# Two modulation slabs at a time between the matmuls of a four-block transformer kernel

## The chip, the cores and the metric

The kernel runs on one core of a Trainium2 chip as one program. The metric is the device time of one execution in microseconds (us); the number given for a kernel is the median of its runs. The engines of the core named below are TensorE (PE, with its weight loads as PEld), VectorE (DVE), ScalarE (ACT), GpSimd (POOL) and SyncE (SP), which here only starts the weight transfers.

## What is computed

Two models of two transformer blocks each, one behind the other, on 256 tokens of 1024 features and a context of 256 more tokens. Every block has an adaptive modulation: a vector `silu(c)` of 1024 numbers for the tokens, and one for the context, is multiplied by a matrix of 1024 x 6144, and the six parts of the result shift, scale and gate what the block does. This product is the subject of the change.

```
def modulation(cvec, w_mod, b_mod):
    m = (jax.nn.silu(cvec) @ w_mod + b_mod).reshape(-1, 1, N_MOD * D_MODEL)
    return jnp.split(m, N_MOD, axis=-1)
...
        x = x + g1 * heads_out(att_x, px, hy, w_out[l])
        x = x + g2 * sq_relu_mlp(modulate(rms_norm(x, norm2_g[l]), sh2, sc2), w_mlp1[l], w_mlp2[l])
...
        mod_x = jnp.split((jax.nn.silu(c) @ ada_w[i] + ada_b[i])[:, None, :], 6, axis=-1)
```

The first model mixes tokens by latent attention (8 heads), a Fourier transform and a long convolution; the second by a gated delta rule and then by gated linear attention. Each block ends in an MLP of 1024 to 4096 to 1024 with a squared ReLU. All is float32.

## The kernel before

**Weights in slabs.** Every weight matrix is cut on the host into slabs of 128 x 2048 float32 (1 MB: 1024 rows by 256 columns), laid in one array in the order in which they are used. SP brings them one after the other into a ring of four places (`ring`, `RING = 4`). In `slabs` the transfer of slab n waits until `n - RING + 2` slabs are begun, that is until slab n-3 has been begun: PE counts `slab_begun` up with the first matmul of each slab, and by then it is through with slab n-4, whose place the new one takes. So when a slab is begun, the transfer of the third slab after it may start.

**Own slabs.** An ordinary product goes in three matmuls (`three_products`, L763 to L765): weights and data are each split into a rounded part and a rest, since the fast format rounds. ACT makes the rounded part of a slab (`w_high`, L1411 in the MLP), DVE the rest (L1894), and only then PE may begin it (`w_split`). In the MLP of both token sets a slab is 48 matmuls of 128x512. ACT makes the rounded part of own slab j+1 only after PE is through with own slab j-1, whose buffer it takes. An MLP runs in four quarters of eight own slabs, 0 to 3 being of the first matrix and 4 to 7 of the second.

**Hosted slabs.** The slabs of the modulation are of another kind. `pe_slab_rows` (L955 to L965; its matmul is L960) multiplies a slab unsplit with two vectors only: eight matmuls, each on 32 columns of the array and in its own quarter of them (`tile_position=(0, r)`). The profile counts each as two, since they are full float32. Four slabs fill one PSUM bank (6); ACT copies it (L1337, L1434), PE turns it (`pe_turn_rows`, L969), DVE adds it up (L976). These slabs depend on nothing near, so they are hosted by other stages. Who hosts them:

- The attention of both blocks of the first model (`pe_attn`), with 24 slabs in its 32 units and 16 slabs in its 16 units (`woven`). A unit is one head and 128 queries: scores of unit i (L990), one hosted slab while i < m, transposes of the probabilities of unit i-2 (L1004), and at even i the products with the values of a pair of units (L1015); at every fourth i also the turn (L969). DVE takes the row minimum (L1735), ACT the exponentials (L1330), DVE scales (L1742), ACT copies the transposes (L1346). In the first 16 units the scores are 512 wide, in the other 16 of the first block 256 wide.
- The MLP of the first block and the MLP behind the delta rule (`hosts`), each with 24 slabs, eight behind the own slabs of each of its first three quarters by `HOSTED`. `mlp_slab` counts where in the ring's order own slab j stands, and `mlp_slabs` on the host lays the slabs in that order. Quarter 0 is written out, quarters 1 and 2 run in a loop, quarter 3 hosts nothing. The turns stand behind own slabs 4 and 7.

```
        HOSTED = ((0,), (1,), (2,), (3,), (4,), (5,), (6, 7), ())
...
            for j in range(6):
                out += [own[j], more[j]]
            out += [own[6], more[6], more[7], own[7]]
```

What sets the order of the work is the text of each engine's program: every engine runs its instructions in order and waits on semaphores. Nothing is scheduled at run time.

Of the kernel before, what the change touches and what calls it, by code (L numbers as in the profile page):

```python
# [233 lines left out]
def build(nc, A, out):  # L234
    with ExitStack() as ctx:
# [178 lines left out]
        freed = [sems[f"freed{b}"] for b in range(8)]  # L414
        landed = [sems[f"landed{s}"] for s in range(RING)]
# [12 lines left out]
        def cs(blk, k, n=0):  # L428

            at = 6 + (blk * KD + k) * 32 - 2 * n  # L430
            return CS[:, at:at + 32]

        def slab_view(s, kt, nc_, off=0):
            return ring[:, s, off:off + kt * nc_].rearrange("p (k n) -> p k n", k=kt)
# [27 lines left out]
        def attn_units(l):  # L462
            return [(s, h, q) for s in range(2 if l == 0 else 1) for h in range(HEADS) for q in range(2)]

        def woven(l):

            rest = [(4 * j, 2 * MT * l + 4 * j) for j in range(8, MOD_SLABS)]
            return rest + ([(4 * j, 2 * MT + 4 * j) for j in range(8)] if l == 0 else [])

        def u_attn(l):  # L470
            n, m = len(attn_units(l)), len(woven(l))
            return {0: n // 2, 1: n // 2, 2: n // 2, 3: n // 2, 4: n // 4, 5: n // 4, 6: m // 4, 7: m // 4, "slab": m,
                    "maxed": n, "scaled": n, "affine": 6, "biased": 1}
# [478 lines left out]
        def keys_of(s):  # L952
            return (0, T2) if s == 0 else (L, L)

        def pe_slab_rows(v, s, blk, n):  # L955

            w = slab_view(s, KD, 256)
            for k in range(KD):
                r = 32 * (k % 4)
                ins = nc.tensor.matmul(ps[r:r + 32, 6, 0:256], cs(blk, k, n % 4), w[:, k, :], start=(n % 4 == 0 and k < 4), stop=(n % 4 == 3 and k >= 4),  # L960
                                       tile_position=(0, r))
                if k == 0:
                    ins.then_inc(sems["slab_begun"], 1)
            if n % 4 == 3:
                ins.then_inc(filled[6], 1)  # L965

        def pe_turn_rows(rows):
            for t in range(2):
                ins = nc.tensor.transpose(ps[:, 7, t * P:(t + 1) * P], rows[:, t * P:(t + 1) * P], ident[:])  # L969
            ins.then_inc(filled[7], 1)  # L970
# [8 lines left out]
        def pe_attn(pe, v, l):  # L979

            units, m = attn_units(l), len(woven(l))
            n = len(units)
            for i in range(n + 3):
                if i < n:
                    s, h, q = units[i]
                    k0, kn = keys_of(s)
                    b = i % 2
                    pe.wait_ge(freed[b], v.free(b, i // 2))
                    q0 = s * L + q * P
                    nc.tensor.matmul(ps[:, b, 0:kn], QT[0:96, h, q0:q0 + P], KT[0:96, h, k0:k0 + kn], start=True, stop=True).then_inc(filled[b], 1)  # L990
                if i < m:
                    s = v.place(i)
                    pe.wait_ge(landed[s], v.landed(i))
                    if i % 4 == 0:
                        pe.wait_ge(freed[6], v.free(6, i // 4))
                    pe_slab_rows(v, s, 0, i)
                if 2 <= i < n + 2:
                    u = i - 2
                    kn = keys_of(units[u][0])[1]
                    b = 2 + u % 2  # L1000
                    pe.wait_ge(freed[b], v.free(b, u // 2))
                    pe.wait_ge(sems["scaled"], v.of("scaled", u + 1))
                    for a in range(kn // P):
                        ins = nc.tensor.transpose(ps[:, b, a * P:(a + 1) * P], PR[:, u % 3, a * P:(a + 1) * P], ident[:])  # L1004
                    ins.then_inc(filled[b], 1)
                if 3 <= i < n + 3 and i % 2 == 0:
                    s, h, q = units[i - 3]
                    k0, kn = keys_of(s)
                    pair, hp = (i - 4) // 2, h // 2 * P
                    b = 4 + pair % 2  # L1010
                    pe.wait_ge(freed[b], v.free(b, pair // 2))
                    for u in (i - 4, i - 3):
                        pe.wait_ge(freed[2 + u % 2], v.freed(2 + u % 2, u // 2 + 1))
                    for a in range(kn // P):
                        ins = nc.tensor.matmul(ps[:, b, 0:L], VT[:, k0 // P + a, hp:hp + P], PT[:, pair % 2, a, :], start=(a == 0), stop=(a == kn // P - 1))  # L1015
                    ins.then_inc(filled[b], 1)
                if 1 <= i <= m and i % 4 == 0:
                    g = i // 4 - 1
                    pe.wait_ge(freed[6], v.freed(6, g + 1))
                    pe.wait_ge(freed[7], v.free(7, g))  # L1020
                    pe_turn_rows(ROWS[:, g % 2, :])
            v.end(u_attn(l))
            pe.drain().then_inc(pe_stage_end, 1)
            pe.wait_ge(act_stage_end, v.stages)
            pe.wait_ge(dve_stage_end, v.stages)
# [97 lines left out]

            return {0: (0,), 2: (1,)}.get(n, ())

        HOSTED = ((0,), (1,), (2,), (3,), (4,), (5,), (6, 7), ())

        def mlp_slab(j, host):

            return j + sum(len(h) for h in HOSTED[:j % 8]) + (j // 8 * 8) if host else j  # L1130

# [14 lines left out]
        def pe_mlp(pe, v, T, norm_next=True, host=()):  # L1146
# [32 lines left out]
            def quarter(i, more, begins=False):  # L1179
                for j in range(8):  # L1180
# [21 lines left out]
                    if host and more:  # L1202
                        if j in (4, 7):
                            pe.wait_ge(freed[6], i * 2 + v.freed(6, j // 7 + 1))
                            pe.wait_ge(freed[7], i * 2 + v.free(7, j // 7))
                            pe_turn_rows(ROWS_MLP)
                        for n in HOSTED[j]:
                            s = v.place(own + 1 + n - HOSTED[j][0])
                            pe.wait_ge(landed[s], v.landed(own + 1 + n - HOSTED[j][0], i, 16))
                            if n % 4 == 0:  # L1210
# [2343 lines left out]
        @block.tensor  # L3554
        def _(pe):
            v = View("pe")
            v.end({})
            pe.drain().then_inc(pe_stage_end, 1)
            pe.wait_ge(act_stage_end, v.stages)
            pe.wait_ge(dve_stage_end, v.stages)  # L3560
            for l in range(DEPTH):
                T = T2 if l == 0 else L
                if l == 0:
                    pe_mod(pe, v)
                pe_in(pe, v, l)
                pe_up(pe, v, l)
                pe_attn(pe, v, l)
                pe_front(pe, v, l)
                pe_out(pe, v, T, MIX_REST)
                pe_mlp(pe, v, T, True, hosts(l))  # L3570
            pe_final(pe, v)
            pe_conv(pe, v)
            pe_delta(pe, v)
            pe_read(pe, v)
            pe_dout(pe, v)
            pe_mlp(pe, v, T2, True, hosts(2))
            pe_gin(pe, v)
            pe_gla(pe, v)
            pe_out(pe, v, L, GMIX_REST)
            pe_mlp(pe, v, L, False)  # L3580
# [53 lines left out]
def slabs_of(w, cols=256, rows=1024):  # L3634

    K, N = w.shape
    out = []
    for c in range(0, N, cols):
        for r in range(0, K, rows):
            blk = w[r:r + rows, c:c + cols]  # L3640
            k, n = blk.shape
            blk = blk.reshape(k // P, P, n).transpose(1, 0, 2)
            if n < cols:
                blk = np.concatenate([blk, np.zeros((P, k // P, cols - n), w.dtype)], 2)
            blk = blk.reshape(P, -1)
            if blk.shape[1] < SLAB:
                blk = np.concatenate([blk, np.zeros((P, SLAB - blk.shape[1]), w.dtype)], 1)
            out.append(blk)
    return out


def mlp_slabs(w1, w2, hosted=()):

    out = []
    for n, q in enumerate(range(0, HT * P, D)):
        own, more = slabs_of(w1[:, q:q + D]) + slabs_of(w2[q:q + D]), hosted[8 * n:8 * n + 8]
        if len(more):
            for j in range(6):
                out += [own[j], more[j]]
            out += [own[6], more[6], more[7], own[7]]  # L3660
        else:
            out += own
    return out
# [23 lines left out]
def second_slabs(I):  # L3687
    conv = slabs_of(I["dn_w_in_2"][0])
    out = conv[:16] + conv[24:] + conv[16:24]
    out += slabs_of(I["dn_w_out_2"][0]) + mlp_slabs(I["ffn_w1_2"][0], I["ffn_w2_2"][0], slabs_of(I["ada_w_2"][1]))  # L3690
    g = I["gla_w_in_2"][0]
    z = np.zeros((D, 16), np.float32)
    low = np.concatenate([g[:, 3072:3088], z, g[:, 3088:3104], z], 1)
    out += slabs_of(g[:, :512]) + slabs_of(low) + slabs_of(g[:, 512:3072])
    return out + slabs_of(I["gla_w_out_2"][0]) + mlp_slabs(I["ffn_w1_2"][1], I["ffn_w2_2"][1])
# [50 lines left out]
```

## Time and profile before

| | us |
|---|---|
| median of 3 runs | 2794.37 |
| lowest and highest run | 2790.46, 2797.18 |
| the profiled execution: its time | 2792.76 |
| the profiled execution: its span | 2790.9 |
| PE busy | 2694.9 (97% of the span) |
| DVE busy, ACT busy | 1615.2, 1191.1 |

How to read it: the span is from the first to the last record of the profile, 1.9 us shorter than the execution's time. The records of PE are pipelined; two matmuls that follow each other overlap in the profile, so the distance between their starts, and not their duration, is what one costs. In rows of a timeline the first number is the start in us from the span's start, the second how long the row lasts, then engine, line, operation, tiles and shapes, and xN where N instructions are merged. A bracket at the end says how long the engine was idle before and for whom.

### The profile page before, as it was taken

The page shows a single profiled execution, that of the slowest core. Times are in us where ns is not written, and L with a number is a line of the kernel's source. Part 1 is how long each engine was busy: PE and PEld are TensorE (multiplying, and loading weights), DVE is VectorE, ACT ScalarE, POOL GpSimd, SP SyncE. Part 2 cuts the span into 40 slices and gives each one's busy share as a digit, 9 for nine tenths or more (in the row PEclk, how much of TensorE's full clock was granted, in tenths as well). Part 3 has the DMA queues.
Part 4 walks back from the last instruction along what each step waited for, and adds up shares of the span by engine and source line. Part 5 has one row for each costly group of instructions (what it writes and reads, how often), then busy time and mean ns, then how long its engine had stood idle before and what let it go on. Part 6 is the DMA issues. An engine that isn't in the chain of part 4 may idle for free.

```text
span 2790.9 us, 44915 instructions
## 1 busy us (share of the span) xinstructions
PE 2694.9 (97%) x17244; PEld 2280.6 (82%) x17244; DVE 1615.2 (58%) x2837; ACT 1191.1 (43%) x2232; POOL 400.7 (14%) x560
## 2 busy tenths in 40 slices
PE   6999999999998999999999999989999999998999
PEld 4756877778857998887789999978777788987999
DVE  4565634334765756985367777784433346457665
ACT  4343522224444445346355556653322234354443
POOL 0000000000000301000066666640000000024000
PEclk9999999999999999999999999999999999999999
DMA  7264244442363543323300000032444433210453
GB/s 292 77 238 154 106 179 164 170 180 95 117 247 138 176 180 136 136 91 110 113 5 1 2 1 2 1 122 100 156 181 169 163 134 134 76 61 32 165 180 136
DMA packets 49628, 343.57 MB, mean 123 GB/s; under 512 B 5296, under 2 KB 7344, under 8 KB 9776
## 3 DMA queue, kind: packets, MB, share of 16 engines
q1 hardware_dynamic: 44960, 324.03, 31.5%
q10 hardware_dynamic: 4496, 17.15, 1.6%
q8 instruction: 120, 1.97, 0.3%
q14 instruction: 52, 0.43, 0.1%
HBM read 333.82 MB, written 7.34 MB: 122 GB/s over the span
## 4 chain that ended last, share of the span: by engine, by line
PE 89%; DVE 6%; ACT 2%; DMA 1%; issue 1%; ACTq 0%; POOL 0%; DVEq 0%; SPq 0%
PE ps L763 21%; PE ps L765 20%; PE ps L764 20%; PE ps L2394 4%; PE ps L960 3%; PE ps L2381 3%; PE ps L2373 2%; PE ps L2402 1%; PE ps L1015 1%; PE ps L990 1%; DVE ring_rest L751 1%; PE ps L2429 1%; PE ps L2446 1%; PE ps L3233 1%; PE ps L2350 1%
## 5 line engine op out<-in xcount | busy, mean ns | idle before, releaser
L763 PE MATMUL ps<-hidden_high,w_high 128*128 128x256 f32 (+2 forms) x1208 | 399.1, 330 | 3.7 <-DVE ring_rest L751 2.2
L1411 ACT ACTIVATE w_high<-ring 128x2048 fp32r<-128x2048 f32 x124 | 236.9, 1911 | 380.7 <-DMA ring<-in_w_dram 257.1
L763 PE MATMUL ps<-h_high,w_high 128*128 128x256 f32 (+1 forms) x1056 | 355.2, 336 | 5.5 <-DVE h_low L737 3.5
L764 PE MATMUL ps<-h_low,w_high 128*128 128x256 f32 (+1 forms) x1056 | 351.8, 333 | 0.0
L764 PE MATMUL ps<-hidden_low,w_high 128*128 128x256 f32 (+1 forms) x1056 | 350.1, 331 | 0.0
L1894 DVE TENSOR_TENSOR mix_high<-ring,w_high 128x2048 fp32r<-128x2048 f32 x56 | 128.4, 2292 | 246.9 <-ACT w_high L1411 246.9
L765 PE MATMUL ps<-hidden_high,ring_rest 128*128 128x256 f32 (+2 forms) x872 | 263.0, 302 | 0.0
L763 PEld LDWEIGHTS ps<-hidden_high,w_high 128*128 128x128 f32 (+1 forms) x1208 | 229.1, 190 | 35.2 <-issue 10.8
L763 PEld LDWEIGHTS ps<-h_high,w_high 128*128 128x128 f32 x1056 | 202.5, 192 | 32.2 <-issue 11.5
L1894 DVE TENSOR_TENSOR ring_rest<-ring,w_high 128x2048 fp32r<-128x2048 f32 x68 | 157.2, 2312 | 123.6 <-ACT w_high L1411 123.6
L764 PEld LDWEIGHTS ps<-h_low,w_high 128*128 128x128 f32 x1056 | 202.6, 192 | 18.2
L764 PEld LDWEIGHTS ps<-hidden_low,w_high 128*128 128x128 f32 x1056 | 200.6, 190 | 18.1
L765 PE MATMUL ps<-hidden_high,mix_high 128*128 128x512 f32 (+1 forms) x544 | 205.0, 377 | 0.0
L765 PE MATMUL ps<-h_high,ring_rest 128*128 128x256 f32 (+1 forms) x672 | 202.1, 301 | 0.0
L765 PEld LDWEIGHTS ps<-hidden_high,ring_rest 128*128 128x128 f32 (+1 forms) x872 | 166.9, 191 | 6.5
L1415 ACT ACTIVATE arena<-ps 128x256 f32<-128x256 f32 (+1 forms) x128 | 62.0, 488 | 244.4 <-PE ps L765 242.9
L765 PE MATMUL ps<-conv_h_high,ring_rest 128*128 128x512 f32 (+1 forms) x392 | 153.4, 391 | 0.0
L763 PE MATMUL ps<-conv_h_high,conv_w_high 128*128 128x512 f32 (+1 forms) x376 | 148.1, 394 | 1.9 <-issue 1.3
L765 PE MATMUL ps<-h_high,mix_high 128*128 128x512 f32 x384 | 149.6, 389 | 0.0
L1816 DVE SCALAR_TENSOR_TENSOR X<-ps,M,X 128x256 f32<-128x256 f32 x224 | 99.0, 478 | 86.8 <-PE ps L765 86.8
L764 PE MATMUL ps<-h_rest,conv_w_high 128*128 128x512 f32 (+1 forms) x376 | 146.4, 389 | 0.0
L1904 DVE TENSOR_TENSOR arena<-arena 128x256 f32<-128x256 f32 (+1 forms) x128 | 73.0, 576 | 125.6 <-ACT arena L1415 125.4
(504 smaller groups left out, 6222.1 us busy)
## 6 DMA issues: line engine op xcount, KB each, us to landing
ring<-in_w_dram SPq DMA_DIRECT2D x302, 1024.0 KB, 4.8
z_spill<-arena ACTq DMA_DIRECT2D x16, 256.0 KB, 2.0
arena<-z_spill SPq DMA_DIRECT2D x2, 2048.0 KB, 9.3
C<-in_first_dram ACTq DMA_DIRECT2D x1, 2432.0 KB, 11.1
X<-in_x_dram ACTq DMA_DIRECT2D x1, 2048.0 KB, 13.0
x_spill<-X ACTq DMA_DIRECT2D x1, 2048.0 KB, 10.1
X<-x_spill SPq DMA_DIRECT2D x1, 2048.0 KB, 7.8
C<-in_third_dram ACTq DMA_DIRECT2D x1, 2048.0 KB, 9.3
```

What stands on the lines that cost most here:

```text
L763: ins = nc.tensor.matmul(out_, w_high, high, start=first, stop=False)
L764: nc.tensor.matmul(out_, w_high, rest, start=False, stop=False)
L765: return ins, nc.tensor.matmul(out_, w_rest, high, start=False, stop=last)
L960: ins = nc.tensor.matmul(ps[r:r + 32, 6, 0:256], cs(blk, k, n % 4), w[:, k, :], start=(n % 4 == 0 and k < 4), stop=(n % 4 == 3 and k >= 4) ...
L1411: nc.scalar.activation(W_HIGH[:, (j + 1) % 2, :], ring[:, s], ACT.Copy).then_inc(sems["w_high"], 1)
L1415: nc.scalar.activation(RELU[:, n % 2, 0:T], ps[:, b, 0:T], ACT.Relu).then_inc(freed[b], 1)
L1816: ins = nc.vector.scalar_tensor_tensor(X[:, n, s * L:(s + 1) * L], ps[:, b, s * L:(s + 1) * L], M[:, 2 * (gate * KD + n) + s:2 * (gate * K ...
L1894: nc.vector.tensor_tensor(mlp_rest(v, j + 1, own, T), ring[:, v.place(own)], W_HIGH[:, (j + 1) % 2, :].bitcast(F32), ALU.subtract).then_in ...
L1904: nc.vector.tensor_tensor(SQR[:, n % 2, 0:T], r, r, ALU.mult).then_inc(sems["squared"], 1)
L2373: ins = nc.tensor.transpose(ps[:, 4 * u, g * P:(g + 1) * P], tt[:, stay * 256 + g * P:stay * 256 + (g + 1) * P], ident[:])
L2381: ins = nc.tensor.matmul(ps[:, 4 * u + 3, g * P:(g + 1) * P], pm_of(u, n)[:, g * P:(g + 1) * P], tt[:, moved * 256 + g * P:moved * 256 + ( ...
L2394: ins = nc.tensor.matmul(ps[:, 4 * u + 1, g * P:(g + 1) * P], unit(u, DT)[:, g * P:(g + 1) * P], unit(u, DT)[:, 256 + g * P:256 + (g + 1) ...
```

## The change

Hosted slabs come in pairs. In attention PE does slabs i and i+1 in unit i where i is even, and none where i is odd. In the hosting MLPs slabs 0 and 1 come behind own slab 1, slabs 2 and 3 behind own slab 3, 4 and 5 behind own slab 5, and 6 and 7 behind own slab 6 as before. The order of the slabs in the array, and so the order of the transfers, follows. Number and kind of all instructions stay; no line of ACT, DVE, POOL or SP is changed, though what they wait for is reached at other times.

```
@@ pe_attn
-                if i < m:
-                    s = v.place(i)
-                    pe.wait_ge(landed[s], v.landed(i))
-                    if i % 4 == 0:
-                        pe.wait_ge(freed[6], v.free(6, i // 4))
-                    pe_slab_rows(v, s, 0, i)
+                if i < m and i % 2 == 0:
+                    for j in range(i, i + 2):
+                        s = v.place(j)
+                        pe.wait_ge(landed[s], v.landed(j))
+                        if j % 4 == 0:
+                            pe.wait_ge(freed[6], v.free(6, j // 4))
+                        pe_slab_rows(v, s, 0, j)
@@ hosts
-        HOSTED = ((0,), (1,), (2,), (3,), (4,), (5,), (6, 7), ())
+        HOSTED = ((), (0, 1), (), (2, 3), (), (4, 5), (6, 7), ())
@@ mlp_slabs
-            for j in range(6):
-                out += [own[j], more[j]]
-            out += [own[6], more[6], more[7], own[7]]
+            out += [own[0], own[1], more[0], more[1], own[2], own[3], more[2], more[3]]
+            out += [own[4], own[5], more[4], more[5], own[6], more[6], more[7], own[7]]
```

PE at the start of attention, before. `arena` holds scores, keys and values; `ring,CS` is a hosted slab with the two vectors.

```order
L990 MATMUL ps<-arena 128x512
L960 MATMUL ps<-ring,CS 32x256 x8
L990 MATMUL ps<-arena 128x512
L960 MATMUL ps<-ring,CS 32x256 x8
L990 MATMUL ps<-arena 128x512
L960 MATMUL ps<-ring,CS 32x256 x8
L1004 MATMUL ps<-ident,arena 128x128 x4
L990 MATMUL ps<-arena 128x512
L960 MATMUL ps<-ring,CS 32x256 x8
L1004 MATMUL ps<-ident,arena 128x128 x4
L990 MATMUL ps<-arena 128x512
```

PE at the same place with the change (its line numbers are one higher behind this place):

```order
L990 MATMUL ps<-arena 128x512
L960 MATMUL ps<-ring,CS 32x256 x16
L990 MATMUL ps<-arena 128x512 x2
L960 MATMUL ps<-ring,CS 32x256 x16
L1005 MATMUL ps<-ident,arena 128x128 x4
L990 MATMUL ps<-arena 128x512
L1005 MATMUL ps<-ident,arena 128x128 x4
L990 MATMUL ps<-arena 128x512
```

Slab 3 has moved from unit 3 to unit 2, slab 1 from unit 1 to unit 0; units 1 and 3 have none left.

PE in quarter 0 of the first hosting MLP, before, where own slab 0 ends (128x256 wide, the last of its matmuls) and own slab 1 begins:

```order
L764 MATMUL ps<-h_low,w_high 128x256
L765 MATMUL ps<-h_high,ring_rest 128x256
L960 MATMUL ps<-ring,CS 32x256 x8
L763 MATMUL ps<-h_high,w_high 128x512
L764 MATMUL ps<-h_low,w_high 128x512
```

With the change, at the same place:

```order
L765 MATMUL ps<-h_high,ring_rest 128x256
L763 MATMUL ps<-h_high,w_high 128x512
L764 MATMUL ps<-h_low,w_high 128x512
L765 MATMUL ps<-h_high,mix_high 128x512
```

and where own slab 1 ends and own slab 2 begins:

```order
L764 MATMUL ps<-h_low,w_high 128x512
L765 MATMUL ps<-h_high,mix_high 128x512
L960 MATMUL ps<-ring,CS 32x256 x16
L763 MATMUL ps<-h_high,w_high 128x512
```

Here own slab 1 follows own slab 0 directly, and hosted slabs 0 and 1 stand together between own slabs 1 and 2.

## Rows read from the trace of the kernel before

**Rows 1.** The page: span, and the chain of work that ended last, by engine.

```profile
span 2790.9 us, 44915 instructions
PE 89%; DVE 6%; ACT 2%; DMA 1%; issue 1%; ACTq 0%; POOL 0%; DVEq 0%; SPq 0%
```

**Rows 2.** Stretches: length, PE, PEld, DVE, ACT, POOL busy, PEclk, DMA share, GB/s.

```profile
340.00:620.00 280.00, 280.00 (x1489) 217.58 (x1488) 104.43 (x137) 72.49 (x76) 0.00 (x0) 1.00 0.46 176
...
170.00:205.00 35.00, 35.00 (x275) 19.65 (x277) 22.06 (x53) 18.40 (x41) 0.00 (x0) 1.00 0.93 350
...
1098.20:1105.00 6.80, 6.20 (x14) 4.46 (x15) 6.80 (x15) 5.22 (x12) 0.00 (x0) 0.50 0.32 108
```

**Rows 3.** Timeline of PE around one hosted slab in the first hosting MLP.

```profile
354.68 0.39 PE L764 MATMUL ps<-h_low,w_high 128*128 128x512 f32 x1
...
362.39 0.39 PE L765 MATMUL ps<-h_high,mix_high 128*128 128x512 f32 x1
...
363.71 0.50 PE L763 MATMUL ps<-h_high,w_high 128*128 128x512 f32 x1
...
365.22 0.39 PE L763 MATMUL ps<-h_high,w_high 128*128 128x512 f32 x1
```

**Rows 4.** Timeline of PE around the two hosted slabs behind own slab 6.

```profile
411.14 0.39 PE L765 MATMUL ps<-hidden_high,mix_high 128*128 128x512 f32 x1
411.46 1.93 PE L960 MATMUL ps<-ring,CS 128*32 128x256 f32 x32
413.33 0.50 PE L763 MATMUL ps<-hidden_high,w_high 128*128 128x512 f32 x1
```

**Rows 5.** Quarter 0, own slab 0 to own slab 1: PE, and DVE's split of own slab 1.

```profile
337.69 0.28 PE L765 MATMUL ps<-h_high,ring_rest 128*128 128x256 f32 x1
337.90 1.07 PE L960 MATMUL ps<-ring,CS 128*32 128x256 f32 x16
339.46 0.50 PE L763 MATMUL ps<-h_high,w_high 128*128 128x512 f32 x1 [0.49 <-DVE mix_high L1894]
...
337.11 2.29 DVE L1894 TENSOR_TENSOR mix_high<-ring,w_high 128x2048 fp32r<-128x2048 f32 x1 [1.19 <-ACT w_high L1411]
```

**Rows 6.** Timeline of ACT: the rounded part of own slab 2 in that quarter.

```profile
343.46 1.92 ACT L1411 ACTIVATE w_high<-ring 128x2048 fp32r<-128x2048 f32 x1 [2.78 <-DMA ring<-in_w_dram]
```

**Rows 7.** Timeline of PE in the first attention: slabs 2 and 4, scores of unit 6.

```profile
168.65 1.07 PE L960 MATMUL ps<-ring,CS 128*32 128x256 f32 x16
...
173.54 1.07 PE L960 MATMUL ps<-ring,CS 128*32 128x256 f32 x16
...
179.43 1.02 PE L990 MATMUL ps<-arena 96*128 96x512 f32 x2
```

**Rows 8.** SP's issue of slab 3, and issue to landing for slab 3 (4.7) and slab 5 (6.3).

```profile
165.26 0.33 SPq L3470 DMA_DIRECT2D ring<-in_w_dram  x1
...
ring<-in_w_dram SPq DMA_DIRECT2D x1, 1024.0 KB, 4.7
...
ring<-in_w_dram SPq DMA_DIRECT2D x1, 1024.0 KB, 6.3
```

**Rows 9.** Timeline of PE: a 256-wide unit with a slab, then units without.

```profile
229.33 0.60 PE L990 MATMUL ps<-arena 96*128 96x256 f32 x2
...
231.14 1.03 PE L1015 MATMUL ps<-arena 128*128 128x256 f32 x4
...
235.69 0.60 PE L990 MATMUL ps<-arena 96*128 96x256 f32 x2
...
236.35 0.60 PE L990 MATMUL ps<-arena 96*128 96x256 f32 x2
237.44 0.41 PE L1004 MATMUL ps<-ident,arena 128*128 128x128 f32 x2 [0.49 <-DVE arena L1742]
```

**Rows 10.** Timeline of PE at the end of the second attention, from the scores of unit 15.

```profile
843.98 1.02 PE L990 MATMUL ps<-arena 96*128 96x512 f32 x2
...
847.48 1.97 PE L1015 MATMUL ps<-arena 128*128 128x256 f32 x8 [0.36 <-ACT arena L1346]
```

## The prediction

> **What bounds the kernel now.** I read the page first, then the stages that the change touches. The chain of work that ended last lies on PE for 89% [rows 1], so what counts is what PE does or waits for. Then the stretches. In the hosting MLP, PE is busy in 280.0 of 280 us at full granted clock, while ACT and DVE have 72 and 104 us of work and the DMA engines are 46% busy. In attention, PE is busy all the time too, but the DMA engines are 93% busy and move 350 GB/s [rows 2]. A slab is 1.0486 MB, so at that rate one lands every 3.0 us. The two kinds of host have to be judged apart: the MLP has only PE as its limit, in attention the transfers stand right behind PE.
>
> **What two hosted slabs cost together and alone, MLP.** One matmul of an own slab costs (362.39 - 354.68) / 34 = 0.227 us, an own slab 48 x 0.227 = 10.9 us [rows 3]. Around a single hosted slab the distance from the last own matmul to the next is 1.32 us, and the next six distances sum to 1.51 where six are 1.36. So a single hosted slab costs 1.32 - 0.23 + 0.15 = 1.24 us [rows 3]. With two in a row the first distance is 2.19 us instead of 1.32 [rows 4]: the second slab costs 0.87, or 0.85 with the rest of the ramp behind. A pair therefore costs 2.09 where two singles cost 2.48, and each merged pair saves 0.40 us. The saving is the way into and out of the 32-column form, paid once instead of twice.
>
> **The MLPs.** There are two hosting MLPs of three hosting quarters. In quarters 1 and 2 three pairs are new (own slabs 1, 3, 5), the fourth was there: 3 x 0.40 = 1.20 us less per quarter. The turn behind own slab 4 now stands alone between own slabs instead of beside a hosted one, which no row prices for slab 4; bounds are 0 and 0.15 more (the ramp once more), and I take 0.06. That gives 4 x 1.14 = 4.6 us less.
> Quarter 0 is different. Before, hosted slab 0 stands in the time in which PE waits for DVE's split of own slab 1: own slab 0 ends with the matmul at 337.69, DVE's split ends at 337.11 + 2.29 = 339.40, and own slab 1 begins at 339.46 although only 0.49 us of that is booked as idle [rows 5]. With the change nothing stands there, PE waits about 1.65 us, and own slab 1 begins at the same 339.46: nothing gained at this place. Hosted slab 0 now costs its 0.85 behind own slab 1. The two other pairs save 0.40 each, less 0.06. Quarter 0: +0.85 - 0.80 + 0.06 = +0.1 us, twice. **MLPs together: -4.6 + 0.2 = -4.4 us**, bounds -4.8 and -4.0.
> What hides the rest: own slab 2 is the fourth slab of the ring behind own slab 0 still, but its transfer is now freed by own slab 1 (begun 339.46) and not by hosted slab 0 (begun 337.90). Before, ACT got it at 343.46, 5.56 us after the slab that freed it [rows 5, 6]. Now that is 339.46 + 5.56 = 345.0, ACT ends at 346.9, DVE 2.3 later at 349.3 with a hand-over, and PE wants it at 339.46 + 10.9 + 2.1 = 352.4. There are 3 us of room. Own slabs 4 and 6 stand the same way (freed by own slabs 3 and 5, two hosted slabs ahead of them); all others are freed by a slab that starts no later in relation to them. ACT's squared ReLU of own slab 1 is queued behind that wait and comes 1.3 us later; its result is wanted in own slab 4 only. If the room were not there, PE would lose what is missing, us for us.
>
> **Attention, the unit.** A 256-wide unit with a slab takes 231.14 - 229.33 = 1.81 us from the scores to the next stage, one without 236.35 - 235.69 = 0.66 [rows 9]. A slab taken out of a unit gives 1.15 us, and put behind another it costs 0.86. So a pair saves 0.29 us where nothing waits. There are 12 pairs in the first attention and 8 in the second.
>
> **Attention, the start.** Here the ring speaks against it. Slab 3 may be fetched when slab 0 is begun. SP issues it at 165.26 and it lands 4.7 later, at 169.96; slab 5, issued about 0.8 after slab 2 is begun (168.65), takes 6.3 since others are in flight, and lands at about 175.7 [rows 7, 8]. Before, slab 3 is wanted in unit 3. Now it is wanted in unit 2 right behind slab 2, which begins at 168.65 as before, since unit 2's scores wait for the first exponentials: slab 3 is wanted at 169.5 and begins at 170.1. From there: 1.0 for the slab, 0.5 for the transposes, 1.3 for unit 3 without a slab, 0.95 for the scores, so slab 4 begins at about 173.9 against 173.54 before. Slab 5 is wanted at 174.75 and has landed at 175.7; it begins at about 175.85, 1.1 us late. Behind it come 1.0 for the slab, 0.5 transposes, 1.73 values, 0.22 turn and 1.31 for unit 5, so the scores of unit 6 start at 180.6 against 179.43 [rows 7]: **+1.2 us**. From slab 6 on the pairs are 6.5 us apart, and a slab in second place has about 6.5 + 0.9 = 7.4 us from its release to its use, against 0.8 + 6.3 = 7.1 when the queue is full and 0.8 + 4.7 = 5.5 when it is empty. That is just enough.
>
> **Attention, the end.** First block: nine pairs from 6/7 to 22/23 save 9 x 0.29 = 2.6. In the last eight units the pairs are only 4.2 to 4.9 us apart, less than two transfers of 3.0 us [rows 2]; the lead that the ring gathered is eaten up, and the last slab comes late. Slab 20 begins at about 224.2, slab 23 may then be fetched and lands 5.5 to 7.1 later, at 229.7 to 231.3, while it is wanted at 229.6: 0.1 to 1.7 late, I take 1.35, as the queue is nearly full. And unit 23 has lost its slab just where the chain over DVE takes over: the transposes at 237.44 start 1.75 after the scores of the unit before (235.69), and PE without slabs is there after 0.66 + 0.44, so 0.65 of what is taken out of unit 23 comes back as a wait [rows 9]. **First attention: +1.2 - 2.6 + 1.35 + 0.65 = +0.6 us.**
> Second block, all 512 wide: the start is the same, +1.2; pairs 6/7 to 12/13 save 4 x 0.29 = 1.2. The last pair 14/15 does not save: it puts 0.86 ahead of the scores of unit 15, and from those scores to the products with the values it takes 3.50 us, ended by ACT's copy of transposes (0.36 of idle) [rows 10]. That chain, minimum, exponentials, copies, doesn't contain slab 15, so it does not get shorter. **Second attention: +1.2 - 1.2 + 0.86 = +0.9 us.**
>
> **The sum.** -4.4 + 0.6 + 0.9 = -2.9 us. The profiled execution took 2792.76 us with a span of 2790.9, so it would take 2789.9. The median of the runs is 1.6 above the profiled one, so I forecast 2794.37 - 2.9 = 2791.5 us. A difference of up to 0.2% (5.6 us) is about what a measurement of this kernel can't tell from none.
>
> **The rivals.**
> *The transfers don't hold attention up.* If a slab always lands 4.7 us after its issue, slab 5 lands at 174.2 before it is wanted, slab 23 at 229.7, and only slab 3 waits. The start then costs 0.1 instead of 1.2, and the end 0.1 instead of 1.35. First attention: +0.1 - 2.6 + 0.1 + 0.65 = -1.75; second: +0.1 - 1.2 + 0.86 = -0.25. Sum: -4.4 - 2.0 = -6.4, 2788.0 us. For it speaks the 4.7 with an empty queue, against it the 6.3 two slabs later [rows 8].
> A page bears on this. The Trainium skill (DMA: Bandwidth & Descriptors, section Bandwidth) measured 425 GB/s for one core with the largest transfers, and names some 358 GB/s as what HBM gives a core when its neighbour streams too. By the first a slab would come every 2.5 us, an estimate from that page, and attention would go as in this rival; by the second every 2.9, as in the forecast. The trace has 350 GB/s at 93% busy engines [rows 2], nearer to the second, so I give the rival little.
> *The transfers hold attention up everywhere: slower.* Slots of the ring are now freed in twos, and if a slab in second place takes its 0.8 + 6.3 = 7.1 us from release to landing even so, pairs can't be closer than 7.1 - 0.86 = 6.2 us. Wide units pass (6.5), but the three distances between the last four pairs of the first attention go from about 4.6 to 6.2: +4.9 instead of the +1.35. If it is 7.7, the wide ones lose their saving too (5 + 4 pairs, 2.6). Sum: -2.9 + 3.5 + 2.6 = +3.2, 2797.6 us. It decides for slower once a slab in second place needs more than about 7.3 us from release to landing. Against it: releases in twos leave the engines emptier when the next one comes.
> *The clock.* New waits of PE of 0.6 to 1.65 us stand in six places. One such place before was followed by 6.8 us at a granted clock of 0.50, 1.2 instead of 2.4 GHz [rows 2]; a stretch like that gives back 3.4 us if PE is the bound. On top of the forecast: 2794.9 us.
> *The change does nothing in the MLP.* Pairs there could be held by the second slab's own wait. Against it: the pair behind own slab 6 ran without a gap [rows 4], and its slabs were fetched as early. Price: +4.4, 2795.9 us.
>
> **How the numbers follow.** Forecast 0.66, transfers no hindrance 0.12, transfers everywhere 0.07, clock 0.10, no gain in the MLP 0.05. Around each stands the spread of a median of runs that lie within 3.4 us of it. The range from 2787 to 2797 holds all but the outer halves of the two transfer cases. Faster by over 0.2% means under 2788.8: most of the second case and a little of the first, 0.14. Slower means over 2800: only two bad cases together, 0.04. Within: 0.82.
>
> **What the profile would show.** Right: groups of 32 records of the hosted line that last 1.93 us, with 2.19 us between the own matmuls around them; waits of PE for the ring at slabs 3 and 5 of both attentions and at slab 23 of the first; about 1.65 us of waiting for DVE's split behind own slab 0 of quarter 0; no wait for own slabs 2, 4 and 6. Wrong: waits of PE for the split in quarters 1 and 2; waits for the ring at many pairs; half clock in attention or behind quarter 0's first own slab; or attention that gets shorter.

## The result, and the profile after

The changed kernel took 2800.3 us (median of 18 runs, 2797.38 to 2805.61) beside 2795.39 for the kernel before (18 runs, 2790.46 to 2799.7), a ratio of 1.0015 with a 95% interval of 1.0009 to 1.0022. Measured once more later (experiment 8) it took 2800.25 us, ratio 1.0019 [1.001, 1.0028]. The forecast was 2791.5 us, with a range from 2787 to 2797. So the change costs 4 to 5 us where a gain of 2.9 was forecast. The profiled execution took 2800.85 us, 8.1 more than that of before.

The page of after, span and chain by engine, answers to [rows 1]. PE's share of the chain has fallen by 3 points, and those of DVE, ACT and DMA have risen:

```profile
span 2799.0 us, 44916 instructions
PE 86%; DVE 7%; ACT 3%; DMA 3%; issue 1%; ACTq 0%; DVEq 0%; SPq 0%; POOL 0%
```

I cut all profiles into the same stages, in us from the start of one stage's first matmul to that of the next's. "Attention" runs from the first scores to the first matmul of the output product behind it. "MLP" runs from own slab 1 of quarter 0 to the start of quarter 3. The last column is the ratio of the timed runs to those of the kernel before, timed beside them. The rows of the experiments are read further down.

| kernel | attention 1 | attention 2 | MLP 1 | MLP 2 | ratio [95%] |
|---|---|---|---|---|---|
| before | 87.7 | 57.1 | 279.2 | 279.3 | 1 |
| after | 94.0 | 60.1 | 277.3 | 277.0 | 1.0015 [1.0009, 1.0022] |
| after, second time | 97.2 | 60.3 | 277.0 | 277.1 | 1.0019 [1.001, 1.0028] |
| mlp_pairs | 87.9 | 57.1 | 277.1 | 277.2 | 0.9989 [0.998, 0.9998] |
| attn_pairs | 92.4 | 62.2 | 279.2 | 279.2 | 1.003 [1.0018, 1.0042] |
| early_copy | 91.6 | 58.2 | 276.9 | 277.1 | 1.0000 [0.9991, 1.0009] |
| odd_units | 87.1 | 55.1 | 276.9 | 276.9 | 0.9983 [0.9974, 0.9992] |
| even_slabs | 95.9 | 61.0 | 274.8 | 274.8 | 1.0001 [0.9992, 1.001] |
| both | 87.3 | 54.9 | 274.8 | 274.8 | 0.9968 [0.9957, 0.9978] |
| mlp_even | 87.8 | 57.0 | 274.8 | 274.8 | 0.9972 [0.9961, 0.9983] |

In after the two MLPs are 1.97 + 2.28 = 4.25 us shorter, as forecast (4.4). The two attentions are 6.4 + 3.0 = 9.4 us longer, where 1.5 was forecast. The difference is +5.1, near the 4 to 5 us of the timed runs. (The profiled execution is 3 us longer than that, mainly because gated linear attention took 75.9 us in it instead of 71.9. In the second profile of the same kernel it took 72.3, so the 4 us belong to one execution and are no part of the change.)

One profile is not enough for a difference of 3 us. The two attentions together take 144.7, 145.0 and 144.9 us in the three profiles that have the attention of before, but 154.1, 157.6, 154.6 and 156.9 in the four that have that of after, where the waits for transfers differ from one execution to the next. So the attentions cost 9.4 to 12.8 us by the profiles; the timed runs of the attention half alone say 8.4.

**The MLPs of after.** PE around a pair behind own slab 1 of quarter 0. The distance between the own matmuls is 2.18 us, beside 2.19 in [rows 4]:

```profile
354.66 0.39 PE L765 MATMUL ps<-h_high,mix_high 128*128 128x512 f32 x1
354.98 1.93 PE L960 MATMUL ps<-ring,CS 128*32 128x256 f32 x32
356.84 0.50 PE L763 MATMUL ps<-h_high,w_high 128*128 128x512 f32 x1
```

And PE between own slabs 0 and 1 of that quarter. The place that [rows 5] shows filled with a hosted slab is now idle:

```profile
342.08 0.28 PE L765 MATMUL ps<-h_high,ring_rest 128*128 128x256 f32 x1
343.86 0.50 PE L763 MATMUL ps<-h_high,w_high 128*128 128x512 f32 x1 [1.49 <-DVE mix_high L1895]
```

PE waits for nothing else in the three hosting quarters.

**Attention of after.** What PE waited for in the first attention: engine, line, releaser, us in total, times, longest.

```profile
PE ps L960 <- ACT arena L1338: 5.0, 5, 1.4
PE ps L1005 <- DVE arena L1743: 2.7, 5, 0.9
PE ps L960 <- DMA ring<-in_w_dram: 2.5, 3, 2.1
PE ps L1016 <- ACT arena L1347: 0.8, 2, 0.6
```

The same view of the kernel before:

```profile
PE ps L1004 <- DVE arena L1742: 2.2, 4, 0.9
PE ps L1015 <- ACT arena L1346: 0.6, 1, 0.6
PE ps L960 <- ACT arena L1337: 0.2, 1, 0.2
```

The first line of after is one that the prediction does not have. The hosted matmuls wait five times for ACT's copy of the bank. In the second attention they wait three times more, 2.2 us. The seed of it was there before: the last line, one wait of 0.2 us, at slab 16. PE in after around slab 8, from the scores of unit 6 on:

```profile
183.85 1.02 PE L990 MATMUL ps<-arena 96*128 96x512 f32 x2
184.72 0.60 PE L1005 MATMUL ps<-ident,arena 128*128 128x128 f32 x4
185.15 1.02 PE L990 MATMUL ps<-arena 96*128 96x512 f32 x2
187.22 1.94 PE L960 MATMUL ps<-ring,CS 128*32 128x256 f32 x32 [1.04 <-ACT arena L1338]
```

The scores at 183.85 are those of unit 7 and those at 185.15 those of unit 8. (Slabs 6 and 7 stood in unit 6, before this excerpt.) Slab 8 opens a new group of four and must wait until ACT has copied the group before. DVE and ACT at that moment:

```profile
184.06 0.43 DVE L1717 COPY arena<-ps 64x256 f32<-64x256 f32 x1 [2.41 <-PE ps L1016]
184.51 0.75 DVE L1729 SCALAR_TENSOR_TENSOR arena<-arena,V 128x510 f32<-128x510 f32 x1
185.30 0.69 DVE L1736 TENSOR_REDUCE arena<-ps 128x1 f32<-128x512 f32 x1
...
186.02 0.69 ACT L1331 ACTIVATE arena<-ps,arena 128x512 f32<-128x512 f32 x1 [2.40 <-DVE arena L1736]
186.61 0.19 ACT L1331 ACTIVATION_READ_ACCUMULATOR arena<-ps,arena 128x1 f32 x1
186.70 0.37 ACT L1338 ACTIVATE arena<-ps 128x256 f32<-128x256 f32 x1
```

The copy itself takes 0.37 us and its data had been ready since slab 7 ended. But in ACT's program it stands behind the exponentials of unit 7, these wait for DVE's row minimum, and that stands in DVE's program behind the copy of the values and a step of the short convolution. From DVE's 184.06 to the end of ACT's copy it is 3.0 us. The kernel before has exactly that chain:

```profile
183.81 0.43 DVE L1716 COPY arena<-ps 64x256 f32<-64x256 f32 x1 [2.03 <-PE ps L1015]
...
186.46 0.38 ACT L1337 ACTIVATE arena<-ps 128x256 f32<-128x256 f32 x1
```

and PE in the kernel before at slabs 8 and 12:

```profile
187.01 1.07 PE L960 MATMUL ps<-ring,CS 128*32 128x256 f32 x16
...
200.49 1.07 PE L960 MATMUL ps<-ring,CS 128*32 128x256 f32 x16
```

There the copy ended at 186.46 + 0.38 = 186.84 and PE reached slab 8 at 187.01, since unit 7 still held a slab of its own. The chain had 0.2 us to spare. The change takes 1.15 us of PE work out of unit 7, which is the unit that covered it.

How much this matters shows in the distance between the first slabs of two groups (8 and 12, four units). Before it was 200.49 - 187.01 = 13.48 us. With the 0.29 that the forecast takes for a pair it would be 13.48 - 2 x 0.29 = 12.90. In after it is 201.23 - 187.22 = 14.01:

```profile
201.23 1.94 PE L960 MATMUL ps<-ring,CS 128*32 128x256 f32 x32 [1.04 <-ACT arena L1338]
```

The ring did hold PE at slab 23, where the forecast put 1.35 us, and behind it a new wait for DVE stands, where it put 0.65:

```profile
234.41 1.07 PE L960 MATMUL ps<-ring,CS 128*32 128x256 f32 x16 [2.09 <-DMA ring<-in_w_dram]
238.25 0.41 PE L1005 MATMUL ps<-ident,arena 128*128 128x128 f32 x2 [0.44 <-DVE arena L1743]
```

### The profile page after: what moved, and what is told of

Same layout as the page of the kernel before. It is cut to its first block, busy times and chain, and to the rows that moved or that the text cites. A ratio compares the mean times of both kernels' runs of the same rounds, so it can differ in the third digit from the quotient of the medians.

```text
span 2799.0 us, 44916 instructions
## 1 busy us (share of the span) xinstructions
PE 2686.7 (96%) x17244; PEld 2289.6 (82%) x17244; DVE 1620.7 (58%) x2837; ACT 1191.7 (43%) x2232; POOL 395.5 (14%) x560
## 3 DMA queue, kind: packets, MB, share of 16 engines
q8 instruction: 120, 1.97, 0.3%
## 4 chain that ended last, share of the span: by engine, by line
PE 86%; DVE 7%; ACT 3%; DMA 3%; issue 1%; ACTq 0%; DVEq 0%; SPq 0%; POOL 0%
PE ps L763 21%; PE ps L764 20%; PE ps L765 20%; PE ps L2395 4%; PE ps L2382 3%; PE ps L960 2%; DMA ring<-in_w_dram 2%; PE ps L2374 2%; PE ps L2403 1%; PE ps L1016 1%; PE ps L2430 1%; DVE ring_rest L751 1%; PE ps L2447 1%; PE ps L2351 1%; PE ps L2437 1%
## 5 line engine op out<-in xcount | busy, mean ns | idle before, releaser
L1416 ACT ACTIVATE arena<-ps 128x256 f32<-128x256 f32 (+1 forms) x128 | 62.2, 489 | 239.0 <-PE ps L765 237.3
```

The lines of the kernel that those rows point to most:

```text
L1416: nc.scalar.activation(RELU[:, n % 2, 0:T], ps[:, b, 0:T], ACT.Relu).then_inc(freed[b], 1)
```

## The experiments

Each kernel is the kernel before or after with one edit. The first four were timed side by side on one chip, the last four on another.

**1. The MLP half alone (mlp_pairs).** The kernel before, with the changed `HOSTED` and `mlp_slabs` and its own attention.

```
-        HOSTED = ((0,), (1,), (2,), (3,), (4,), (5,), (6, 7), ())
+        HOSTED = ((), (0, 1), (), (2, 3), (), (4, 5), (6, 7), ())
```

> Pairs in the two hosting MLPs only; attention is that of the kernel before. Theory A (the MLPs gain what the rows said, attention alone loses): 4.1 to 4.4 us less than before, ratio 0.9985; the time from the end of the first attention to the scores of the second is 2.0 us shorter, as in the changed kernel. Rival B (the MLPs gain nothing, what looks like it is one run against another): 0, ratio 1.000.

Measured: 2791.32 us, ratio 0.9989 [0.998, 0.9998], some 3 us less than before. Both MLPs are 2.1 us shorter in the profile (see the table), attention is as before. The interval leaves out rival B's 1.000, if not by much, and holds theory A's 0.9985. So the MLP term of the forecast, -4.4, holds: -4.2 by the stages, and within the interval of the runs.

**2. The attention half alone (attn_pairs).** The kernel before, with pairs in even units and the MLPs untouched.

```
-                if i < m:
-                    s = v.place(i)
...
+                if i < m and i % 2 == 0:
+                    for j in range(i, i + 2):
+                        s = v.place(j)
```

> Pairs in attention only; the MLPs are those of the kernel before. Theory A: attention alone costs what its two stretches grew by, 6.4 and 3.0 us: 9.4 us more than before, ratio 1.0034. Rival B: attention costs the whole difference between the two kernels and no more, about 4.9 us, ratio 1.0018.

Measured: 2803.01 us, ratio 1.003 [1.0018, 1.0042], 8.4 us more than before. Theory A's 1.0034 lies inside the interval, rival B's 1.0018 at its very end. The two halves add to the whole change: 0.9989 - 1 + 1.003 - 1 = +0.0019. The bank waits are the same in number and size as in after:

```profile
PE ps L960 <- ACT arena L1338: 5.0, 5, 1.4
PE ps L960 <- DMA ring<-in_w_dram: 1.3, 3, 0.6
```

The second attention of this profile is 2.1 us longer than that of after. PE waited 0.5 us longer for slab 5, and 3.4 us at a granted clock of 0.50 followed. All of the loss is in attention.

**3. The bank copied one unit earlier (early_copy).** The changed kernel with one condition of ACT altered: the copy of the bank stands behind the exponentials of unit 4g+2, not 4g+3. The four slabs of the group are done by then, since slabs 4g+2 and 4g+3 both stand in unit 4g+2.

```
-                if i < m and i % 4 == 3:
+                if i < m and i % 4 == 2:
                     g = i // 4
                     act.wait_ge(filled[6], v.filled(6, g))
```

> The changed kernel with one thing moved: ACT copies the full bank of four hosted slabs (L1337 before) in unit 4g+2, where with pairs its fourth slab is done, instead of in unit 4g+3. Theory C (PE loses its time to the bank: the first slab of the next four waits until ACT has copied it, and that copy stands behind the exponentials of a unit that now begins only 1.3 us earlier): the eight waits for the copy, 7.2 us together, go, and the time is about 2 to 3 us under that of before, ratio 0.999. Rival D (the ring holds attention up anyway, and the wait for the bank only stands in front of it): waits for the ring take their place at slabs 4, 8, 12, the time stays 3 to 5 us over before, ratio 1.0015.

Measured: 2795.32 us, ratio 1.0000 [0.9991, 1.0009], 4 us less than after by the ratios. The bank waits are gone. PE at slabs 8 and 12:

```profile
187.98 1.93 PE L960 MATMUL ps<-ring,CS 128*32 128x256 f32 x32
...
200.88 1.93 PE L960 MATMUL ps<-ring,CS 128*32 128x256 f32 x32
```

That is 12.90 us apart, just what 0.29 us a pair gives. So the bank copy's place in ACT's order causes the 14.01. But of the 7.2 us of bank waits only 4.3 come back in the stages (2.5 and 1.8, against the first profile of after), for PE now reaches some slabs before they have landed. So the time came out between theory C (0.999) and rival D (1.0015): C has the cause, and D has what takes back part of the gain. What PE waited for at the ring in the first attention, where after has 2.5 us:

```profile
PE ps L960 <- DMA ring<-in_w_dram: 5.4, 5, 1.6
```

One of the five is the wait at slab 5 that the forecast expected (1.1 us):

```profile
175.95 1.07 PE L960 MATMUL ps<-ring,CS 128*32 128x256 f32 x16 [1.62 <-DMA ring<-in_w_dram]
```

The first profile of after has no such wait in its first attention. Its second profile has one of 1.81 us, so it is not the bank wait ahead that decides this.

**4. The pairs in odd units (odd_units).** The changed kernel, where unit i takes slabs i-1 and i if i is odd. The first slab of a group then stands one unit later, in unit 4g+1.

```
-                if i < m and i % 2 == 0:
-                    for j in range(i, i + 2):
+                if i < m and i % 2 == 1:
+                    for j in range(i - 1, i + 1):
```

> The changed kernel with the pairs of attention in the odd units: slabs i-1 and i in unit i. The copy of the bank is not moved, but the next four slabs start two units after it is made, and slab 3 is wanted where it was before. Theory C: no wait for the bank and none for the ring at slabs 3 and 5; a pair saves its 0.29 us; the last slab of the first attention waits 1 to 2 us for the ring. First attention 1.5 to 2 us shorter than before, second about 1.5, with the MLPs about 7 us under before, ratio 0.9975. Rival D: the ring is what limits: the pairs wait for it, attention is no shorter than before or longer, ratio 0.9985 or above.

Measured: 2789.12 us, ratio 0.9983 [0.9974, 0.9992], 5 us less than before and 9 less than after by the ratios. The interval holds both theory C's 0.9975 and rival D's 0.9985, so the profile has to decide. It has no bank wait, and ring waits at slabs 22 and 23 alone. The first attention:

```profile
PE ps L1005 <- DVE arena L1743: 2.2, 4, 0.9
PE ps L960 <- DMA ring<-in_w_dram: 1.6, 2, 1.4
...
PE ps L990 <- ACT arena L1331: 0.3, 1, 0.3
```

A pair in an odd unit comes later than its two slabs came on average, in an even one earlier. That gives the copy one more unit, and at the start the ring too: there is no wait at slabs 3 and 5. Against before, the attentions are 0.5 and 1.9 us shorter in the profile, and nearly the same in the profile of the kernel with both edits (0.4 and 2.1). At the scores of unit 22 the first is 2.3 us ahead of before, and it gives 1.8 back at the last pair, which waits 1.6 us for the ring. The 1.5 to 2 expected for it had a wait of 1 to 2 us in it and was still too high.

**5. The pairs behind even own slabs (even_slabs).** The changed kernel, its attention untouched.

```
-        HOSTED = ((), (0, 1), (), (2, 3), (), (4, 5), (6, 7), ())
+        HOSTED = ((0, 1), (), (2, 3), (), (4, 5), (), (6, 7), ())
...
+            for j in range(0, 8, 2):
+                out += [own[j], more[j], more[j + 1], own[j + 1]]
```

> The changed kernel with its attention left alone, and the pairs of the hosting MLPs put behind own slabs 0, 2, 4 and 6 instead of 1, 3, 5 and 6. Theory E (a wait that hides a slab is worth as much as a merge): in quarter 0 PE waits 1.49 us for DVE's split behind own slab 0 when nothing stands there. The pair stands there now and hides it: own slab 1 begins 2.19 us after the last matmul of own slab 0, about 0.4 us later than it did, and the pair costs nothing elsewhere, where it cost 2.09. So 1.65 to 1.9 us less per hosting MLP than the changed kernel, quarters 1 and 2 as they are: 3.3 to 3.8 us less than the changed kernel in all, each hosting MLP 275.1 to 275.4 us from the first own matmul of own slab 1 of quarter 0 to quarter 3 as far as the stage's start is counted alike, 2796 to 2797 us. Rival F (the split is what counts, it only moves): own slab 1's transfer is now freed by own slab 0 and not earlier, its split comes later by as much, PE waits behind the pair, and nothing is gained: 2800 us. Attention keeps its bank waits of 7.2 us under both.

Measured: 2795.82 us, ratio 1.0001 [0.9992, 1.001], beside 2800.25 for after on the same chip. Theory E holds. Each MLP is 274.83 us long, to the hundredth in all three kernels with this edit (275.1 to 275.4 was expected), and PE waits for nothing in it. The wait of 1.49 us behind own slab 0 is filled, as the profile of the kernel with both edits shows:

```profile
337.45 0.28 PE L765 MATMUL ps<-h_high,ring_rest 128*128 128x256 f32 x1
337.66 1.93 PE L960 MATMUL ps<-ring,CS 128*32 128x256 f32 x32
...
339.52 0.50 PE L763 MATMUL ps<-h_high,w_high 128*128 128x512 f32 x1
```

From own slab 0 to own slab 1 it takes 2.07 us instead of 1.78, and the pair costs nothing elsewhere. From the last matmul of own slab 0 to quarter 3 it is 2.07 + 274.83 = 276.90, in after 1.78 + 276.98 = 278.76 (second MLP): 1.86 less, at the upper end of what was expected.

**6. Both edits (both).** Odd units and even own slabs.

> Pairs of attention at odd units and pairs of the MLPs behind even own slabs. If the two edits act on different stages and each is what I take it for, their gains add: the kernel with odd units alone came to 0.9983 of the kernel before (4.8 us less), and theory E gives 3.3 to 3.8 more: 0.9970, about 2786 us, in a profile no bank waits, no wait for a split behind own slab 0 of quarter 0. By rival F it is the same as odd units alone, 0.9983, 2789.5 us.

Measured: 2785.94 us, ratio 0.9968 [0.9957, 0.9978]. The edits add. This kernel beats before by 9 us and after by 14.

**7. Even own slabs, attention as before (mlp_even).**

> The attention of the kernel before (one slab in each unit), and the pairs of the MLPs behind even own slabs. It tells what pairs are worth in attention when they are at the right place. In the profile of the kernel with odd units both attentions together were 2.4 us shorter than before. If that is real, this kernel takes about 2.4 us more than the one with both (0.9978, 2788.3 us). If it is only half clock that one profile had and the other had not, the two are equal within 0.5 us. Against the kernel before: pairs alone in the MLPs measured 0.9989, theory E makes this 0.9976 to 0.9978, rival F 0.9989.

Measured: 2787.05 us, ratio 0.9972 [0.9961, 0.9983]. By the table the MLPs are 4.4 us shorter each. But there own slab 1 begins 2.07 us behind the last matmul of own slab 0, where before it was 1.77, ahead of where the stage is counted from. So the gain is 4.1 us each, 8.2 in all, against 7.8 by the ratio. Beside the kernel with both edits it is 1.1 us slower, with intervals that overlap widely. The profiles say 2.6 for the attentions (87.82 + 57.04 against 87.29 + 54.94), with no stretch at half clock in any of these four. The runs neither confirm nor exclude that. So nearly all of the gain lies in the MLPs, and pairs in attention at the better of the two places tried are worth 1 to 3 us.

**8. The changed kernel again (after_again).**

> The changed kernel once more, beside the others on the same chip, and with a second profile. Its one profile had gated linear attention 4 us longer than any other and more half clock. If that is the chance of one execution, this profile has that stage at 71.8 to 72.4 us as all others have it, the bank waits of PE again at slabs 4, 8, 12, 16 and 20 of the first attention and 4, 8, 12 of the second with 6.5 to 7.5 us in all, and a ratio to the kernel before of 1.0009 to 1.0022 as measured. If the stage is again at 76, the change reaches further than into the stages that host slabs.

Measured: 2800.25 us, ratio 1.0019 [1.001, 1.0028]. The bank waits are again 5.0 and 2.2 us, and gated linear attention took 72.3 us. Attention 1 however was 97.2 us long, 3.2 more than in the first profile. Its waits for the ring were 2.1 us longer, and behind the one at slab 23 the granted clock fell. The stretch behind that wait, in this profile and then in the first (columns as in [rows 2]):

```profile
237.80:241.20 3.40, 3.19 (x20) 1.75 (x21) 0.00 (x0) 0.39 (x1) 0.00 (x0) 0.50 0.95 311
```

```profile
234.20:237.60 3.40, 3.19 (x28) 2.20 (x28) 0.81 (x3) 0.38 (x1) 0.00 (x0) 1.00 0.95 316
```

The wait ahead of it was 2.23 us in the one and 2.09 in the other. From the start of slab 23 to the end of the stage it is 22.58 us in this profile and 21.10 in the first: the stretch at half clock (1.2 instead of 2.4 GHz) goes with some 1.5 us more.

## Why the prediction was wrong

- **The step that failed** is the one called "Attention, the unit": "a pair saves 0.29 us where nothing waits", used in nine and four places as if nothing waited there, with "slab 4 begins at about 173.9" as its first use. I followed the ring's semaphore, and left out the second one, which the diff itself shows beside it: `freed[6]`, at every fourth slab. It holds eight of the twenty pairs, for 0.66 to 1.39 us, 7.2 us in all, where before had 0.2. The groups of four that were to be 0.58 us shorter became 0.53 longer (14.01 against 13.48). The waits view of before has the line with 0.2 us in it, and the prediction makes nothing of it. Here that small wait was the sign that the cover ended there. Of the 7.9 us by which the two attentions of the first profile missed their forecast, the bank is 7.0 and slab 23 another 0.7. As a price of the bank alone the 7.0 is too high: with its waits gone, the ring took part of the time (experiment 3).
- **The same question, asked for half of the units only.** For unit 23 I did see that a slab taken out uncovers DVE's chain (0.65). That reasoning holds for every unit that loses its slab, and I used it for the last one alone.
- **Attention, the start:** forecast +1.2 from the ring alone. Measured from the first scores to those of unit 6, the first profile has 178.43 - 161.48 = 16.95 us against 179.43 - 163.44 = 15.99: +0.96, of which 0.66 was the bank at slab 4 and 0.26 the ring at slab 3. That this is near the forecast is chance. Over the eight attentions of the four profiles with pairs in even units it is +0.96 to +3.7, mostly +1.5 to +1.9: 0.66 for the bank each time, 0.26 to 0.66 for the ring at slab 3, and 0 to 1.81 at slab 5. The ring's part was right in kind, and the bank was missing beside it.
- **Attention, the end:** slab 23 was forecast 1.35 late and was 2.09, 2.23 and 2.12 late in three profiles, and only 0.26 in the fourth, attn_pairs. Its transfer was issued 0.8 us after slab 20 began in all four, as the forecast has it, but took 6.8, 6.9 and 6.8 us to land in the three and 4.9 in attn_pairs. The mechanism is right; what makes the same transfer 2 us slower stays open. The 0.65 of DVE behind it measured 0.44 for DVE and 0.28 for ACT's copy after it. In the second attention the last pair gained nothing, as forecast: the transposes behind it waited 1.07 us for DVE.
- **The MLPs:** -4.4 forecast, -4.25 measured, each term visible: pairs at 2.18, a wait of 1.49 for the split in quarter 0, none for own slabs 2, 4 and 6. A quarter of the loop took 97.11 us before and 96.03 to 96.10 in the first MLP of after, and 95.9 in other kernels with these pairs: at best the full 1.20 of three pairs, so that the 0.06 for the turn was not needed.
- **The rivals.** None of them was this. "Transfers hold attention up everywhere" had the right sign and the right stage with the wrong resource. Its price (+3.2) came near the measured one by accident. The range ended at 2797 since each rival was priced apart. The two attentions came out 7.9 us above their forecast, more than any single case allowed. The clock rival had a part in some executions: of the eight attentions, three have a stretch at half clock. Behind the wait of quarter 0 no profile has one. The 0.82 for a time within 0.2% of before came true by the ratio (0.15% more), but only because a gain of 4 us and a loss of 9 stood against each other.

A page of the Trainium skill has the rule that I should have weighed. Perfetto Trace Analysis, section Optimizing Tensor Performance, wants matmul groups to rotate through several PSUM banks, so that the copy of one overlaps the matmuls of the next. Here all groups of four use bank 6, and the trace agrees: the next group stands 1.04 us until a copy of 0.37 us is done. Two banks for the groups were not tried. The early copy took those waits away in another way, and there the ring took up part of the gain.

## What to carry to other kernels

Filler work that is moved out of a place uncovers whatever it covered there. Go through every wait of the engine at the place that loses it, each semaphore and not the likeliest alone, and read the small waits of the profile too: 0.2 us at one of five groups was all that showed of a copy that had no more than 0.2 us of room at slab 8. Where work has to be paired, the side of the pair matters more than the pairing (even or odd units: 9 us here, the merge itself 1 to 3), and the best place for a filler is a wait that exists anyway. A small copy that frees a buffer should be queued as soon as its data are there, and not behind a step that waits for a third engine.

## What was new about the hardware

- Of the stretches at a granted clock of 0.50, six stand at the same place of the program in all ten profiles (near 900, 1100, 1850, 2485, 2570 and 2600 us), 3.4 to 10.2 us long. Others come and go between executions. Behind the wait for slab 23 there was one after 2.23 us (and one after 2.12, in even_slabs) and none after 2.09. With such a stretch of 3.4 us it took 22.58 and 22.47 us to the end of the stage, without one 21.10: 1.4 to 1.5 us.
- The same transfer of 1 MB, issued at the same place of the same schedule, landed after 6.8 to 6.9 us in three profiles and after 4.9 in the fourth. Together with the clock this makes differences of one to three us between profiles of equal stages, and a stage has to be read in two profiles before a difference of that size means anything.
- The merge of two hosted slabs saved its 0.29 us in attention and 0.40 in the MLP, as read from rows of single and double slabs, to within 0.01 us: 12.90 us from slab 8 to slab 12 in the three kernels without bank waits (13.48 before, two pairs), and 95.91 us for a quarter of the loop (97.11 before, three pairs) in odd_units.
